# Moving three side-input gate tiles out of the expert loop and to its front, on alternating PSUM bank pairs

## The reference: one layer with attention, an mLSTM, sixteen experts and a gated side input

```python
ff = hier_moe(h, w_grp[l], b_grp[l], w_exp[l], b_exp[l], w_gate[l], w_up[l], w_down[l])
ple = (p[l] @ w_ple[l]) * jax.nn.sigmoid(h @ w_ple_gate[l])
h = layer_norm(DN_ALPHA * h + ff + ple, ln2_g[l], ln2_b[l])
```

```python
hg = jnp.einsum('td,edf->tef', xt, w_gate)
hu = jnp.einsum('td,edf->tef', xt, w_up)
h = jax.nn.silu(hg) * hu * combine[:, :, None].astype(hg.dtype)
return jnp.einsum('tef,efd->td', h, w_down).reshape(B, S, D)
```

## Time and profile before

| | |
|---|---|
| median of 3 runs | 1613.43 us (1612.69 to 1613.9) |
| the profiled execution's own time | 1613.67 us |
| its span, first to last instruction | 1611.9 us |
| granted TensorE clock, mean | 0.984 |
| PE busy | 1501.9 us (93%) |
| DVE / ACT / POOL busy | 659.7 / 494.5 / 67.7 us |
| HBM read | 391.69 MB |
| ring stage, from the first gate matmul to the last down slot's start | 979.86 to 1574.10 us |

### The profile page before, as it was taken

How to read it: one execution, slowest core, us unless ns; L and a number is a source line. 1 busy time by engine, 2 the same in 40 slices (tenths; PEclk the granted TensorE clock), 3 DMA queues, 4 the chain that set the end, 5 groups by cost and what they waited for, 6 DMA issues and landing times.

```text
span 1611.9 us, 16579 instructions
## 1 busy us (share of the span) xinstructions
PE 1501.9 (93%) x6640; PEld 1000.9 (62%) x6640; DVE 659.7 (41%) x896; ACT 494.5 (31%) x662; POOL 67.7 (4%) x69
## 2 busy tenths in 40 slices
PE   8999999999999999999999989979988998898872
PEld 6887888887778888888888856423423532342221
DVE  5546665466566554545456544000111021011116
ACT  4444444455544444444444323100200100020011
POOL 0000000046000000000000020000000000000001
PEclk9999999999999999999999998999999999999996
DMA  8654555554434556555659451697999799879991
GB/s 291 190 175 157 181 163 200 163 174 140 153 122 144 182 190 201 183 199 191 195 185 348 165 188 52 278 419 298 373 422 411 299 376 422 350 316 422 422 401 57
DMA packets 130250, 394.83 MB, mean 245 GB/s; under 512 B 11264, under 2 KB 13952, under 8 KB 105600
## 3 DMA queue, kind: packets, MB, share of 16 engines
q1 hardware_dynamic: 121600, 384.45, 64.6%
q10 hardware_dynamic: 8576, 9.36, 1.7%
HBM read 391.69 MB, written 2.10 MB: 244 GB/s over the span
## 4 chain that ended last, share of the span: by engine, by line
PE 80%; DMA 17%; DVE 1%; ACTq 1%; issue 1%; ACT 0%; SPq 0%; POOL 0%; DVEq 0%
PE bank L449 18%; PE bank L450 18%; PE bank L454 17%; DMA moe_ring<-in_w_gate_dram 9%; PE bank L805 7%; PE bank L849 7%; DMA moe_ring<-in_w_down_dram 4%; PE bank L880 4%; DMA moe_ring<-in_w_ple_gate_dram 3%; PE bank L829 2%; PE bank L744 1%; PE bank L779 1%; PE bank L476 1%; PE bank L607 1%; PE bank L629 1%; DMA w_ring<-in_w_in_dram 1%
## 5 line engine op out<-in xcount | busy, mean ns | idle before, releaser
L1411 DVE TENSOR_TENSOR w_lo<-w_ring,w_hi 128x1024 fp32r<-128x1024 f32 (+1 forms) x312 | 381.9, 1226 | 307.4 <-ACT w_hi L1017 306.5
L1017 ACT ACTIVATE w_hi<-w_ring 128x1024 fp32r<-128x1024 f32 (+1 forms) x312 | 327.2, 1050 | 317.0 <-PE bank L454 309.3
L449 PE MATMUL bank<-w_hi,xT_hi 128*128 128x512 f32 (+1 forms) x864 | 347.3, 402 | 2.3 <-ACT w_hi L1017 2.3
L450 PE MATMUL bank<-w_hi,xT_lo 128*128 128x512 f32 (+1 forms) x864 | 335.9, 389 | 0.0
L849 PE MATMUL bank<-moe_ring,xg 128*64 128x512 f32 x1024 | 231.0, 597 | 35.4 <-DMA moe_ring<-in_w_gate_dram 18.2
L454 PE MATMUL bank<-w_lo,xT_hi 128*128 128x512 f32 (+1 forms) x864 | 229.4, 387 | 0.0
L449 PEld LDWEIGHTS bank<-w_hi,xT_hi 128*128 128x128 f32 x864 | 162.7, 188 | 38.8 <-issue 7.1
L849 PEld LDWEIGHTS bank<-moe_ring,xg 128*64 128x64 f32 x1024 | 69.9, 137 | 183.3 <-issue 130.3
L450 PEld LDWEIGHTS bank<-w_hi,xT_lo 128*128 128x128 f32 x864 | 163.0, 189 | 32.6 <-issue 1.9
L454 PEld LDWEIGHTS bank<-w_lo,xT_hi 128*128 128x128 f32 x864 | 161.8, 188 | 33.4
L880 PE MATMUL bank<-moe_ring,moe_hiddenT 128*64 128x512 f32 x448 | 103.3, 606 | 17.2 <-DMA moe_ring<-in_w_down_dram 17.2
(11 more groups left out here) (265 smaller groups left out, 1372.4 us busy)
## 6 DMA issues: line engine op xcount, KB each, us to landing
w_ring<-in_w_in_dram SPq DMA_DIRECT2D x104, 1024.0 KB, 5.0
moe_ring<-in_w_gate_dram SPq DMA_DIRECT2D x32, 2048.0 KB, 15.0
moe_ring<-in_w_up_dram SPq DMA_DIRECT2D x32, 2048.0 KB, 15.6
moe_ring<-in_w_down_dram SPq DMA_DIRECT2D x32, 2048.0 KB, 16.1
w_ring<-in_w_proj_a_dram SPq DMA_DIRECT2D x16, 1024.0 KB, 5.0
w_ring<-in_w_proj_m_dram SPq DMA_DIRECT2D x16, 1024.0 KB, 5.1
w_ring<-in_w_out_dram SPq DMA_DIRECT2D x16, 1024.0 KB, 5.1
moe_ring<-in_w_ple_gate_dram SPq DMA_DIRECT2D x8, 2048.0 KB, 16.8
```

The costliest lines, as they stand in the source:

```text
L449: mm(b, lh(k, m), WH[:, s, kk, 0:width], start=start and kk == 0, stop=False)
L450: mm(b, ll(k, m), WH[:, s, kk, 0:width], start=False, stop=False)
L1017: fn(WH[:, h % 4, :, 0:width], W32[:, h // 2, 2 * (h % 2):2 * (h % 2) + 2, 0:width], ACT.Copy).then_inc(hi_ready, 1)
L1411: v.tensor_tensor(WL[:, h % 4, :, 0:width], W32[:, h // 2, 2 * (h % 2):2 * (h % 2) + 2, 0:width], WH[:, h % 4, :, 0:width].bitcast(F32), A ...
```

## The change

The list is written anew: the four gate tiles are its first four entries, and the experts' up and down entries follow in their old order with nothing between. So all eight gate slots come first through the ring. Tile j now uses banks 2/3 for even j and 0/1 for odd j. With two bank pairs in turn, tile j from j = 2 on waits until the sigmoid of tile j - 2 has read them. `gather(0)`, which writes banks 0/1, stands behind tile 3 instead of tile 0 and waits for `ple_sig` 4, the sigmoid of tile 3. up(1), which writes banks 2/3, waits for `ple_sig` 3. The waits of tiles 1 to 3 for `e_Tc` and `y_add` go, and so does the wait of gather(1) to gather(3) for a gate tile's sigmoid. ACT runs its four `ple_gate` and DVE its four `ple_part` in a row, ahead of the first gather's work on ACT and the first pair's on DVE. No instruction that computes is added or removed.

```diff
-ORDER = (("ple", 0), ("up", 0), ("up", 1), ("ple", 1), ("down", 0), ("up", 2), ("down", 1), ("up", 3), ("ple", 2),
-         ("down", 2), ("up", 4), ("down", 3), ("up", 5), ("ple", 3), ("down", 4), ("up", 6), ("down", 5), ("up", 7),
+ORDER = (("ple", 0), ("ple", 1), ("ple", 2), ("ple", 3), ("up", 0), ("up", 1), ("down", 0), ("up", 2), ("down", 1),
+         ("up", 3), ("down", 2), ("up", 4), ("down", 3), ("up", 5), ("down", 4), ("up", 6), ("down", 5), ("up", 7),
          ("down", 6), ("down", 7))
...
             def ple_tile(j, after=None):
 
-                b = 0 if j else 2
+                b = 2 * ((j + 1) % 2)
+                if j >= 2:
+                    pe.wait_ge(ple_sig, j - 1)
...
                 if n == 1:
-                    pe.wait_ge(ple_sig, 1)
+                    pe.wait_ge(ple_sig, 3)
...
                     if k == 2 and n % 2 == 0 and n < NP - 2:
-                        pe.wait_ge(ple_sig, n // 2 + 2)
                         gather(n // 2 + 1)
...
             ple_tile(0, after=lambda k: expert_counts() if k == 11 else None)
             pe.wait_ge(bank_free[0], 21)
+            for j in range(1, 4):
+                ple_tile(j)
+            pe.wait_ge(ple_sig, 4)
             gather(0)
-            for kind, n in ORDER[1:-1]:
+            for kind, n in ORDER[4:-1]:
                 if kind == "up":
                     up(n, (lambda i: turn_pair(0) if i == 2 else None) if n == 1 else scatter_after(n - 2) if n else None)
-                elif kind == "down":
+                else:
                     down(n, down_after(n))
-                else:
-                    if n == 1:
-                        pe.wait_ge(e_Tc, 1)
-                    else:
-                        pe.wait_ge(y_add, 2 * CHUNKS * (2 * n - 2))
-                    ple_tile(n)
...
-            ple_gate(0)
+            for j in range(4):
+                ple_gate(j)
             group_tables(0)
             gathered(0)
...
-            ple_part(0)
-            for kind, n in ORDER[1:-1]:
-                if kind == "ple":
-                    if n > 1:
-                        dv.wait_ge(y_add, 2 * CHUNKS * (2 * n - 2))
-                    ple_part(n)
-                elif kind == "up":
+            for j in range(4):
+                ple_part(j)
+            for kind, n in ORDER[4:-1]:
+                if kind == "up":
```

More of the change, by code:

```diff
@@ L1345, in y_part @@
                 fn(ygh[:, c, :], B[c if n == NP - 1 else 4 + c][:, :], ACT.Copy).then_inc(y_hi, 1)
-            ple_gate(0)
+            for j in range(4):
+                ple_gate(j)
             group_tables(0)
             gathered(0)
-            for kind, n in ORDER[1:]:
-                if kind == "ple":
-                    ple_gate(n)
-                elif kind == "up":
+            for kind, n in ORDER[4:]:
+                if kind == "up":
                     if n == 1:
```

## The result

| | before | changed |
|---|---|---|
| first comparison, median us | 1613.66 (4 runs, 1612.69 to 1614.56) | 1622.56 (4 runs, 1622.23 to 1624.92) |
| second comparison | 1614.59 (25 runs, 1611.89 to 1619.38) | 1619.89 (8 runs, 1619.01 to 1622.99) |
| profiled execution, own time; span | 1613.67; 1611.9 | 1622.4; 1620.6 |
| PE busy | 1501.9 (93%) | 1509.1 (93%) |
| granted clock, mean | 0.984 | 0.980 |

The ratio is 1.0058 (95% interval 1.0041 to 1.0076) in the first comparison and 1.0037 (1.0023 to 1.0050) in the second. The change makes the kernel slower by 5 to 9 us; 6.6 were predicted. One execution of a later kernel, 2567.03 us long at a mean granted clock of 0.555, is left out of the medians and ratios here.

The account below looks back on a forecast made before the run. PE in gate tiles and gathers, and loads elsewhere, were taken to bound the ring stage in turn. Front tiles +83.1, sigmoid wait +1.6 and loop -78.1 gave +6.6 us, so 1620.0 us, range 1616.0 to 1624.0.

Parts of the forecast that it names:

- Three tiles at the front, +83.1: Ahead of the first gather: PE is full, so each moved tile adds its 27.70 us, without load or bank waits.
- The wait for the last sigmoid, +1.6: Before the first gather: PE now waits for tile 3's sigmoid, +1.6 us, with nothing to hide it.
- the sum: Whole kernel: +83.1 + 1.6 - 78.1 = +6.6 us, giving 1620.0 us.
- A rule against the change: Load-bound loop: the skill's rule has DMA waits between short matmul groups throttle the clock repeatedly; taken at nothing.
- The tiles leave the loop, -78.1: Loop periods: each falls from 146.44 to 120.4 us without its tile, giving back 26.0 us, three times.
- the gather's loss of 1.1 us: Gathers in the loop: PE frees no ring place meanwhile, so about 1.1 us of load time is lost per gather.
- The pace: Load-bound loop slots: one load per 4.97 us, so 24 slots take 119.3 us.
- The whole tile given back: Loop rival: no gather loss, each tile gives back 27.2 us; no measurable change, about 1615.8 us; chance 0.16.
- The faster case: Loop rival: expert slots come quicker than 4.97 us; at 4.80 us the time is 1607.7 us; chance 0.05.
- the loss of rate: Long load-bound stretch, rival: loads slow to 5.1 us a slot, about 1629 us; chance 0.05.
- The clock rival: Long load-bound stretch: the clock falls repeatedly; four drops in the ups add 6 us, 1626 us; chance 0.06.

Follow-up runs that it names:

- The direct weighing: The changed kernel with gate tiles 1 to 3 left out (loads, products, sigmoids, additions): 1538.59 us, ratio 0.9527 to before.
- the last kernel: From before: gate tiles cut into one-slot halves, placed away from the gathers, and gathers cut in three: 1589.70 us, ratio 0.9841.

## Why the prediction was right

The direction, the mechanism and the range held: 1622.56 and 1619.89 against 1620.0 (1616.0 to 1624.0). That the second median lies 0.1 us from the forecast is luck: the ring stage was longer by 8.5 and 9.0 us, not 6.6, and the part ahead of the ring happened to be shorter. By its steps:

- **Three tiles at the front, +83.1.** Measured 88.95 - 6.55 = 82.4, or 27.47 us per tile. The 27.70 of the earlier trace rows runs to the end of the tile's last product, past the start of the next group; from start to start it is 1121.15 - 1093.52 = 27.63. No bank wait and no load wait stood between them: PE was busy 83.70 of 83.70 us.
- **The wait for the last sigmoid, +1.6.** Measured 1.73, and shown by moving tile 3 to its own banks. What the sum lacked is the lower clock in the gather behind it, +1.2 us (12.26 for 11.05). This was the weak step: "A rule against the change" looked for the clock in the load-bound stretch, and took it at nothing. The first of the two stretches ran at 1.00; the clock fell in gathers, and once in down(3), where a slot took 5.35 us behind a wait of 2.05 (1365.93), like the one drop of the earlier trace rows.
- **The tiles leave the loop, -78.1.** For the first two tiles 26.0 and 25.9 us, predicted 26.0, with the gather's loss of 1.1 us shown by cutting the gather. The pace was 4.97 us. The third gave only 24.3 to 24.5. There the gather is long, from one down slot to the next 1323.97 - 1308.89 = 15.08 us for 13.66, and the window inside it reads 0.53. The two rows of PE's timeline, and the window:

```profile
1308.89 3.65 PE L882 MATMUL bank<-moe_ring,moe_hiddenT 128*64 128x512 f32 x16 [0.73 <-DMA moe_ring<-in_w_down_dram]
...
1323.97 3.65 PE L882 MATMUL bank<-moe_ring,moe_hiddenT 128*64 128x512 f32 x16
```

```profile
1315.50:1318.90 3.40, 3.40 (x19) 3.40 (x18) 0.00 (x0) 1.20 (x2) 0.00 (x0) 0.53 1.00 414
```

- **Two late slots, not in the sum, and in the end no cost.** In up(1) of the changed kernel, PE's timeline reads:

```profile
1132.52 3.65 PE L851 MATMUL bank<-moe_ring,xg 128*64 128x512 f32 x16 [1.32 <-DMA moe_ring<-in_w_up_dram]
1137.58 3.65 PE L851 MATMUL bank<-moe_ring,xg 128*64 128x512 f32 x16 [1.41 <-DMA moe_ring<-in_w_gate_dram]
1143.26 3.65 PE L851 MATMUL bank<-moe_ring,xg 128*64 128x512 f32 x16 [2.03 <-DMA moe_ring<-in_w_up_dram]
1148.95 3.65 PE L851 MATMUL bank<-moe_ring,xg 128*64 128x512 f32 x16 [2.04 <-DMA moe_ring<-in_w_gate_dram]
1153.77 3.65 PE L851 MATMUL bank<-moe_ring,xg 128*64 128x512 f32 x16 [0.57 <-DMA moe_ring<-in_w_up_dram]
```

Two starts lie 5.68 and 5.69 us apart instead of 4.97, together 1.4 us. They only take back a lead. With tile 3 on its own banks the same pair is there (5.48 and 5.77), yet the first stretch is 96.49 us, as without the tiles (96.47): up(0)'s seventh slot starts 32.05 us behind the gather's start there, 33.42 without the tiles. So the 1.2 us by which the changed kernel's first stretch (97.66) is longer are the first gather's clock. The second slot of up(1) is late in all five traces with a moved tile at the front (5.48 to 5.84), the third in three of them; in the four with up(0) right behind a whole tile 0 the second is not (4.76 to 4.88). The DMA engines were full meanwhile (share 1.01). Why the loads land late is open.

- **The sum.** In the first pair of traces +84.13 - 24.8 - 26.1 - 24.5 - 0.2 = +8.5, where +6.6 was predicted. The front came out 0.6 us under the prediction (84.13 for 84.7), the loop gave back 2.5 too little (75.6 for 78.1). What was mis-sized is the clock, taken at nothing: 1.2 us in the first gather, whose stretch is the loop's first, and 1.4 us in gather(2). Only the first was tested by an experiment; the second is read from rows. It is slow in both traces of the changed kernel, and no gather in the loop is in either trace of before; why gather(2) and not the others is open. The direct weighing says the same: 83.44 at the front against 74.95 in the loop.
- **The rivals.** The whole tile given back (27.2 each) is excluded by the 26.0. The faster case and the loss of rate are excluded by 4.97 us and 414 to 422 GB/s. The clock rival had its place wrong and its size partly right: two gathers lost 1.2 and 1.4 us. The Trainium skill (TensorE: Matmul & The Clock Gate, "HAM oscillation — how this bites in real kernels") has the chip throttle again and again where a group of matmuls is shorter than the wait for DMA behind it. The prediction applied this to the new stretch, and that was a misreading: here a group takes 3.65 us and the wait 1.3 us, so the page's case is not met, and the mean of 1.00 over 120.35 us does not contradict it. Nor does it cover the single windows at 0.51 to 0.57: none of the waits just ahead of them was longer than 2.40 us. Of the rate, 414 to 422 GB/s in the loop, the Trainium skill has it otherwise: about 358 GB/s per core, half of what it gives for the two cores that share a stack of HBM (DMA: Bandwidth & Descriptors, "Specifications"). Here one core ran alone, and the measurement decides.
- **A small misreading.** The prediction has the DMA row at 7 to 9 from slice 26 on; slice 26 itself reads 6. Nothing in the sum uses it.

## What to carry to other kernels

Where PE-bound and load-bound work alternate through one ring, the PE-bound part pays for itself only as far as the ring lets the loads run on beneath it: a block that is moved costs its length at the place where it goes, and gives back at the place it leaves only the difference between the stretch as it is and the time that the remaining loads take alone. Bunching it at the front makes two stages that each idle the other resource (+5 to +9 us here); cutting it to the size of one ring slot and keeping it away from other PE bursts does the opposite (-24 us with no less work). When a wait of a microsecond or two is added just ahead of PE work, look at the granted clock behind it too.

## What was not expected of the hardware

- The clock fell behind quite short waits. In the changed kernel the first gather started 1.73 us later (its row shows PE idle for 1.18 us), and ran at 0.51; without that wait the same gather ran at 1.00 (11.06 for 12.26 us). Ahead of the loop's slots, over all twelve traces, none of 346 waits for a load of 1.0 to 1.99 us had a slot at the lower clock behind it, 16 of 30 waits of 2.00 to 2.42 us had, and all 8 of 2.48 to 4.33 us. In between, the length of the wait does not decide. Two one-slot tiles of the last kernel show it:

```profile
1151.02 15.73 PE L807 MATMUL bank<-moe_ring,h1T 128*128 128x256 f32 x64 [2.34 <-DMA moe_ring<-in_w_ple_gate_dram]
...
1431.97 14.05 PE L807 MATMUL bank<-moe_ring,h1T 128*128 128x256 f32 x64 [2.41 <-DMA moe_ring<-in_w_ple_gate_dram]
```

- The pace of a 2 MB load goes with the length of its contiguous rows: 4.97 us with rows of 8 KB (expert tiles), 5.5 us with 2 KB (a whole gate tile's first slot, 1088.01 to 1093.52) and about 6.0 us with 1 KB (256-column gate tiles, 1216.09 to 1222.14). The last pair's down weights show the same beside the others, being read in rows of 2 KB; in the trace of before the starts lie 5.33 and 5.40 us apart, with PE waiting for the load:

```profile
1563.07 3.65 PE L899 MATMUL bank<-moe_ring,moe_hiddenT 128*64 128x512 f32 x16 [0.54 <-DMA moe_ring<-in_w_down_dram]
...
1568.47 3.65 PE L899 MATMUL bank<-moe_ring,moe_hiddenT 128*64 128x512 f32 x16 [0.62 <-DMA moe_ring<-in_w_down_dram]
```

- Executions of one program differ by about 3 us ahead of the ring, though each stage behind it repeats within some tenths: gather(3) stands at 430.61 and 430.64 in two traces of the changed kernel.
